# Recurrent mixer of a hybrid decoder layer: consumers of VectorE's drains wait on the drains' own counter

## What is computed

```python
a_mat = jnp.where(strict, jnp.einsum('bnhid,bnhjd->bnhij', k_beta, k) * decay, 0.0)
t_inv = lax.linalg.triangular_solve(eye + a_mat, eye, left_side=True, lower=True)
attn = jnp.einsum('bnhid,bnhjd->bnhij', q, k) * decay
def step(state, xs):
    v_new = u_c - jnp.einsum('bhik,bhkv->bhiv', w_c, state)
    o = jnp.einsum('bhik,bhkv->bhiv', q_c, state) + jnp.einsum('bhij,bhjv->bhiv', attn_c, v_new)
    state = state * jnp.exp(gl_c)[..., None, None] + jnp.einsum('bhik,bhiv->bhkv', k_c, v_new)
```

## Time and profile before

| | us |
|---|---|
| median of 3 runs | 597.84 |
| the runs | 596.25, 597.97, 597.84 |
| profiled execution, its own time | 597.7 |
| span of the profiled execution | 595.8 |
| TensorE matmul busy | 545.4 (92%) |
| VectorE busy | 390.1 (65%) |
| ScalarE busy | 322.1 (54%) |
| GpSimd busy | 221.1 (37%) |

### The profile page before, as it was taken

One profiled execution on the slowest core, in us unless ns is written; L12 is line 12 of the kernel. 1 busy time (PEld: TensorE's weight loads), 2 busy tenths in 40 slices (PEclk: granted clock), 3 DMA queues, 4 the chain that ended last, 5 costly groups with the idle time before them and its releaser, 6 DMA issues.

```text
span 595.8 us, 10710 instructions
## 1 busy us (share of the span) xinstructions
PE 545.4 (92%) x4087; PEld 308.0 (52%) x4087; DVE 390.1 (65%) x920; ACT 322.1 (54%) x573; POOL 221.1 (37%) x164
## 2 busy tenths in 40 slices
PE   2999999999999866999899998989899898999997
PEld 1644556543357532467466575645455465444443
DVE  6520388765498696876877768668797556687211
ACT  4555645355467962560922805586676768246320
POOL 0154453613046660352632630441321375154420
PEclk9999999999999996999999999999999999999999
DMA  9345865653124230220220210212211221172411
GB/s 316 114 125 137 167 96 162 189 164 89 56 54 125 75 107 33 72 72 2 73 72 2 64 45 2 59 49 72 72 36 38 70 72 37 36 282 72 142 53 54
DMA packets 31173, 52.93 MB, mean 89 GB/s; under 512 B 2743, under 2 KB 13329, under 8 KB 31121
## 3 DMA queue, kind: packets, MB, share of 16 engines
q1 hardware_dynamic: 30825, 51.68, 29.9%
q10 hardware_dynamic: 296, 0.55, 0.5%
HBM read 49.80 MB, written 2.42 MB: 88 GB/s over the span
## 4 chain that ended last, share of the span: by engine, by line
PE 68%; DVE 17%; ACT 7%; issue 5%; SPq 2%; DMA 1%; POOL 0%; DVEq 0%; ACTq 0%; PEldq 0%; POOLq 0%
PE bank L1690 13%; PE bank L1692 12%; PE bank L1691 12%; PE bank L1986 5%; PE bank L1988 5%; PE bank L1896 5%; PE bank L1990 5%; PE bank L1888 3%; PE bank L1726 3%; ACT stage L744 2%; PE bank L1832 2%; DVE bank L1266 1%; DVE early L1300 1%; DVE small L1297 1%; ACT late L966 1%
## 5 line engine op out<-in xcount | busy, mean ns | idle before, releaser
L532 POOL TENSOR_TENSOR w_lo<-stage,w_hi 128x1024 f16<-128x1024 f32 (+4 forms) x76 | 149.4, 1970 | 218.9 <-ACT w_hi L752 218.8
L752 ACT ACTIVATE w_hi<-stage 128x1024 f16<-128x1024 f32 (+4 forms) x76 | 74.5, 981 | 13.9 <-PE bank L1692 9.0
L1986 PE MATMUL bank<-hT_hi,w_hi 128*128 128x512 f16 x192 | 73.0, 380 | 1.7 <-PE bank L1990 0.9
L744 ACT ACTIVATE stage<-stage,small 128x512 f32<-128x512 f32 (+4 forms) x120 | 73.6, 663 | 0.7 <-DMA stage<-in_w_in 0.6
L1988 PE MATMUL bank<-hT_lo,w_hi 128*128 128x512 f16 x192 | 72.9, 380 | 0.3
L1990 PE MATMUL bank<-hT_hi,w_lo 128*128 128x512 f16 x192 | 72.8, 379 | 0.3
L1690 PE MATMUL bank<-w_hi,hT_hi 128*128 128x260 f16 (+4 forms) x192 | 61.4, 320 | 3.0 <-DVE hT_lo L1074 1.4
L1691 PE MATMUL bank<-w_lo,hT_hi 128*128 128x260 f16 (+4 forms) x192 | 61.0, 318 | 0.0
L1692 PE MATMUL bank<-w_hi,hT_lo 128*128 128x260 f16 (+4 forms) x192 | 61.0, 318 | 0.0
L1690 PE MATMUL bank<-hT_hi,w_hi 128*128 128x512 f16 (+1 forms) x128 | 48.0, 375 | 2.5 <-ACT work L735 1.4
L1691 PE MATMUL bank<-hT_lo,w_hi 128*128 128x512 f16 (+1 forms) x128 | 47.8, 373 | 0.0
(11 more groups left out here) (331 smaller groups left out, 1145.9 us busy)
## 6 DMA issues: line engine op xcount, KB each, us to landing
stage<-in_w_in SPq DMA_DIRECT2D x40, 512.0 KB, 3.6
stage<-in_c_phi_w SPq DMA_DIRECT2D x8, 512.0 KB, 4.1
stage<-in_w_branch SPq DMA_DIRECT2D x8, 512.0 KB, 3.8
stage<-in_w_out SPq DMA_DIRECT2D x8, 512.0 KB, 4.7
stage<-in_w_in SPq DMA_DIRECT2D x8, 260.0 KB, 2.8
strips<-rel_rows SPq DMA_DIRECT2D x8, 256.0 KB, 6.5
late<-in_x SPq DMA_DIRECT2D x1, 2048.0 KB, 9.1
out_x<-late SPq DMA_DIRECT2D x8, 256.0 KB, 2.0
```

What stands on the lines that cost most here:

```text
L532: gp.tensor_tensor(piece_view(w_lo[:, k % PAIRS, :], c), piece_view(stage[:, piece_at[c, j] % STAGES, :], c), piece_view(w_hi[:, k % PAIRS ...
L744: ins = nc.scalar.activation(full[:, r, :], full[:, r, :], ACT.Copy, scale=g_w[:, 2 * j + r:2 * j + r + 1])
L752: nc.scalar.activation(piece_view(w_hi[:, k % PAIRS, :], c), full, ACT.Copy).then_inc(hi_ready, 1)
L1986: mm(G.bank(g)[:, :], w[0], h[0], start=k == 0, stop=False)
```

## The change

`GD`, its list of names and `done` go. Each waiter now waits for the same drain on `v_drained` itself, through a table that turns the old names into those of the ring. VectorE no longer waits behind a drain, and raises nothing there. One wait is kept, as `taken`: in chunk 0, ahead of predicated copies that read `neg_nT`. In `level_zero` of a later chunk, `transposed_zero` (two predicated copies into `t_hT`, the second held) moves ahead of the two predicated copies into `t_h`, of which the last raises `v_drained` for `n`. All 98 calls of `done` go; the waits of TensorE, ScalarE and GpSimd keep their places.

```diff
-        GD = Steps(sem("deltanet_ready"), g_names)
+        drain_of = {"nnt": "kk", "attn": "qk", "tt0": "n", "t": "u", "tt": "ut", "resid": "ks", "kt": "vt", "vnew": "x2", "oraw": "o", "state": "st"}
+
+        def drained(eng, kind, *at):
+            eng.wait_ge(v_drained, V.filled((drain_of.get(kind, kind), *at)))
...
-                GD.wait(gp, ("oraw", c))
+                drained(gp, "oraw", c)
...
-                        GD.wait(act, ("tt", c, LEVELS - 2))
+                        drained(act, "tt", c, LEVELS - 2)
...
-            def done(name):
-
+            def taken(name):
                 ve.wait_ge(v_drained, V.filled(name))
-                ve.nop().then_inc(GD.sem, 1)
...
                 ve.tensor_tensor(neg_nT, bank4(("kk", c)), decay_n, ALU.mult).then_inc(v_drained, 1)
-                done(("kk", c))
                 ve.tensor_tensor(attnT[c % 2], bank4(("qk", c)), attnT[c % 2], ALU.mult).then_inc(v_drained, 1)
-                done(("qk", c))
                 if c == 0:
+                    taken(("kk", 0))
                     transposed_zero(0)
...
                 ps = bank4(("n", c))
+                if c:
+                    transposed_zero(c)
                 put(t_h, 0, ps[0:HALF, :, 0:HALF], 0, HALF)
                 put(t_h, 0, ps[HALF:P, :, HALF:P], HALF, P).then_inc(v_drained, 1)
-                if c:
-                    transposed_zero(c)
-                done(("n", c))
...
                     ve.tensor_copy(z_h[r0:P, :, :], ps[r0:P, :, :]).then_inc(v_drained, 1)
-                    done(("z", c, l))
...
                         put(t_h, l, halves4(("u", c, l))[0:r1, :, :], 0, r1).then_inc(v_drained, 1)
-                        done(("u", c, l))
                         put(t_hT, LEVELS - 1 + l, halves4(("ut", c, l))).then_inc(v_drained, 1)
...
-                    done(("ut", c, l))
...
-                    GD.wait(pe, ("z", c, l))
+                    drained(pe, "z", c, l)
                     if l > 1:
-                        GD.wait(pe, ("tt", c, l - 1))
+                        drained(pe, "tt", c, l - 1)
...
-                        GD.wait(pe, ("state", c - 1))
+                        drained(pe, "state", c - 1)
```

More of the change, by code:

```diff
@@ L671, in _ @@
                 if c < NT - 1:
-                    GD.wait(gp, ("z", c, LEVELS - 1))
+                    drained(gp, "z", c, LEVELS - 1)
                     reset(t_h)
-                    GD.wait(gp, ("tt", c, LEVELS - 1))
+                    drained(gp, "tt", c, LEVELS - 1)
                     gp.wait_ge(joined, c + 1)
@@ L934, in _ @@
                     if c > 1:
-                        GD.wait(act, ("oraw", c - 1))
+                        drained(act, "oraw", c - 1)
                     for h in range(4):
@@ L978, in _ @@
             drain_gate(11)
-            GD.wait(act, ("oraw", NT - 1))
+            drained(act, "oraw", NT - 1)
             for u, (m, q, h) in enumerate(units):
@@ L1381, in token_major @@
                 ve.tensor_tensor(v_tok, bank4(("vt", c)), heads(nk, c), ALU.mult).then_inc(v_drained, 1)
-                done(("vt", c))
             def decayed_products(c):
@@ L1523, in _ @@
                         ins.then_inc(v_drained, 1)
-                        done(("ks", c))
                         next(norm)
@@ L1537, in _ @@
                 ve.tensor_tensor(v_new, bank4(("x2", c)), heads(a_s, c), ALU.mult).then_inc(v_drained, 1)
-                done(("x2", c))
                 if c < NT - 1:
@@ L1550, in _ @@
                     ve.tensor_tensor(o_tok, ps, o_state, ALU.add).then_inc(v_drained, 1)
-                done(("o", c))
                 if c < NT - 1:
@@ L1560, in _ @@
                         ins.then_inc(v_drained, 1)
-                    done(("st", c))
                     token_major(c + 1)
@@ L1968, in within_b2 @@
                 if (t, k) == (3, 1):
-                    GD.wait(pe, ("nnt", 0))
+                    drained(pe, "nnt", 0)
                     transposes(("n", 0), [neg_nT[:, h, :] for h in range(4)])
@@ L2039, in _ @@
                 qc, kc_, vc_ = features(c)
-                GD.wait(pe, ("tt0", c))
+                drained(pe, "tt0", c)
                 for l in range(1, LEVELS):
@@ L2065, in _ @@
                         fill(FILL_U)
-                        GD.wait(pe, ("t", c, l))
+                        drained(pe, "t", c, l)
                 if c < NT - 1:
@@ L2070, in _ @@
                     fill(8)
-                GD.wait(pe, ("tt", c, LEVELS - 1))
+                drained(pe, "tt", c, LEVELS - 1)
                 pe.wait_ge(joined, c + 1)
@@ L2075, in _ @@
                     fill(FILL_X)
-                    GD.wait(pe, ("nnt", c + 1))
+                    drained(pe, "nnt", c + 1)
                     transposes(("n", c + 1), [neg_nT[:, h, :] for h in range(4)])
@@ L2081, in _ @@
                     compressed_out()
-                GD.wait(pe, ("vnew", c))
+                drained(pe, "vnew", c)
                 four(("o", c), lambda h: attnT[c % 2][:, h, :], lambda h: v_new[:, h, :])
```

## The result

| | before | after |
|---|---|---|
| median of five runs, us | 597.84 | 594.21 |
| the runs | 596.25, 596.75, 597.84, 597.93, 597.97 | 592.45, 592.9, 594.21, 594.43, 594.84 |
| profiled execution: own time, span | 597.7, 595.8 | 594.84, 592.9 |
| VectorE busy | 390.1 | 385.1 |

The ratio is 0.994, with a 95% interval of 0.9918 to 0.9963: faster by 3.6 us, where 2.1 was forecast.

A forecast was written before the change was run, and what follows sets the result against it. TensorE holds 68% of the chain, VectorE 17%; freeing VectorE pays only where it stands on the chain, in the recurrent stage. Five terms sum to 2.09 us, so 597.84 becomes 595.7, range 594.3 to 597.8.

The forecast's parts named there:

- The price of a `done`: VectorE's wait for its own drain plus a NOP costs 0.23 us if what follows waits for nothing else.
- Term 1: Two releases on the chain, first transposes before the stage and first `z` of chunk 0: 0.03 each, 0.06 us.
- Term 2: Chunk 0 to 1: `k_tok` starts earlier behind the state's copy, the first `z` waits for it: gain 0.20 us.
- rival B: Less won: the gap falls only to the held 0.04, 0.11 a piece, chunk 1 stays blocked; 597.0 us, chance 0.20.
- Term 3: Chunk 1, cumulative product and levels 3 to 5, where VectorE runs against GpSimd: gain 0.85 us (0.23 to 1.49).
- both blocked: Chunk 1: lines 1036 and 1424 stay held by GpSimd, only the level 4 `z` copy's `done` counts: 0.23 us.
- both escape: Chunk 1: lines 1036 and 1424 are no longer held by GpSimd, all is won: 1.49 us.
- Terms 4 and 5: Chunk 2's cumulative product gains 0.29 us; chunk 3, `resid` to level 3's `z` copy, three `done`s gain 0.69.
- rival A: More won: both blocked chunk 1 operations escape and the pause before 364.05 goes with the NOP; 594.7 us, chance 0.15.
- Rival C: VectorE's gap is the operation's own and stays; only releases gain, 0.03 at some eight places; 597.6 us, chance 0.14.
- Rival D: Slower: VectorE's earlier operations meet GpSimd's in a worse order in chunks 1 and 2; 600.8 us, chance 0.06.
- The margin of `st`: `level_zero`'s new order delays the drain of `n`, but hides before `st`'s loads with some 0.1 us left.

The follow-up runs named there:

- Which drains: Changed kernel with wait and NOP put back behind all drains but resid, z, u and state: 594.59 us; counterpart, put back behind only those: 596.43.

## Why the prediction was right and wrong

*The price of a `done`, 0.23.* Right behind `resid` and the `z` copies: -0.09 in after, and the three kernels split it into 0.11 for the wait and 0.12 for the NOP behind it.

*Term 1, releases.* The kernel with its `done`s kept and its consumers moved shows 0.06, as forecast.

*Term 2, `k_tok`.* 0.12 for 0.20. `k_tok` starts 0.03 behind the state's copy and not under it; here rival B's assumption holds. `v_tok` now also stands 0.03 behind `k_tok`, but for another reason: it waits for TensorE's transposes, which end at 276.90 + 0.66 = 277.56. After's timelines of TensorE and VectorE:

```profile
276.90 0.66 PE L1707 MATMUL bank<-consts,qkvT 128*128 128x128 f32 x4 [0.24 <-DVE late L1537]
277.60 0.69 DVE L1372 TENSOR_TENSOR work<-bank,small 128x512 f32<-128x512 f32 x1
```

In before, too, `v_tok` started 0.04 behind those transposes, so the row from which the prediction took its -0.08 could not show it. The value was right: in the kernel with the 48 freed the transposes end at 277.04, and `v_tok` at 277.43 starts 0.08 under the end of `k_tok`.

*Term 3, chunk 1.* The largest step inside the terms: 1.07 for 0.85, inside its bounds of 0.23 to 1.49. The middle was a compromise between "both blocked" and "both escape". What happened is one of each. Line 1031 was blocked in the place of 1036, line 1412 won its race. Of the 1.49, 0.42 stayed behind: the 0.32 above the floor at 293.50, and 0.09 that TensorE lost at a gate product before it. The margin of 0.02 is no luck of hundredths. In after line 1411 is itself held until GpSimd's operation ends, and 1412 gets in ahead of GpSimd's next; in the traces of all eight runs that keep GpSimd's order and where 1412 wins, it wins by 0.02.

*Terms 4 and 5.* 0.31 for 0.29 and 0.73 for 0.69, at the forecast loads.

*The step that failed: two pauses that the sum puts at nothing.* The sum took 0.23 a `done` and the releases, and nothing else. It left out 0.72 from two pauses of VectorE ahead of a put. The one at 364.05 was seen, and left to rival A with 0.15, as a thing that goes with the NOP. The one at 319.06 was not seen at all: its put is marked as waiting for TensorE, and chunk 2's levels had been read as standing at their floor, though the load there had 0.72 ahead of it. The runs showed in its place that these pauses do not belong to the `done`. With all 98 kept and one instruction more on the list, both are gone, 0.73 us; they stand at numbers 579 and 707 of VectorE's list, behind a wait or NOP by itself. The change takes 97 instructions off the list and moves both puts. That no other operation on the chain met such a number in its place is in part luck: the kernel with 48 freed lost 0.34 that way. With both pauses in the sum the forecast would have been 2.8 us, and 595.0. What such a pause is stays open.

*The rest, in small steps, 0.24 for 0.06.* In the kernel that keeps its `done`s the releases give 0.06, so 0.18 of it is VectorE's. It is not traced to single operations; one source can be the second put of a pair, which starts under the first one's end (0.84 for two puts where they took 1.03).

*From 3.2 to 3.6.* The stage gives 3.2. In the runs whose stage is shorter by 3.16 to 3.20, the medians differ from before's by 3.2 to 3.8, and in the repeat of after itself by 3.3. So the 0.4 beyond the stage is variation, most likely that ahead of the stage, and no gain of the change. Without it the time would have been inside the range.

*Rival C* falls: wait and NOP cost what they seemed to, the NOP alone nothing. *Rival B* holds at `k_tok`. *Rival A* was nearest, with its pause gone, though not by way of the NOP, and only one of its two blocked operations free. *Rival D*'s mechanism is real, with the sign turned: in the kernel with two NOPs it is the later VectorE that fell behind one more GpSimd operation in chunk 1 and lost the race of chunk 2, 1.5 us together. *The margin of `st`* was enough.

## What to carry to other kernels

A semaphore raised by the working instruction itself cost nothing that shows here: the next operation starts 0.08 us under its end. A wait placed on the producer's own sequencer so that it may raise another one costs 0.11 us for the wait and 0.12 for what is issued behind it, wherever that engine is on the chain. Look for gaps that are longer than others of the same kind before summing a per-item price, also where the view names another engine as the releaser. A change of a program's length moves such stalls by itself, so a control with one idle instruction more is worth its run. And the price of speeding an engine up is not that of slowing it down: 0.23 less per drain gave 2.4 us in the stage, 0.09 more took over 4, of which 1.5 was collisions and some new pauses.

## What the runs showed of the hardware

VectorE paused by 0.34 to 0.37 us ahead of instructions 451, 579, 707 and 835 of its list, 128 apart, waits and lone NOPs counted. It showed at six places in three programs, each time right behind a wait or a lone NOP. At 579 in the two kernels of "Which drains", behind a wait but with an operation still running, only 0.05 of it is left. At number 451 of the kernel with 13 NOPs, behind a working instruction, nothing showed; nor did it at 835 of the kernel with one instruction more, behind a wait and under an operation that still ran. One NOP more moved three of them off, and 0.73 us went. By the Trainium skill (Runtime: NRT & Kernel Launch, section Instruction fetch mechanics) an engine refills its instructions in blocks of 256 and the crossing is mostly hidden. A spacing of 128 does not agree with blocks of 256, and no run here shows whether these pauses are fetches.

Two operations of VectorE and GpSimd that meet: the one that starts first keeps its time, even by 0.02 us, and the other is stretched. It is 0.69 to 1.45 or 1.50 on VectorE, 1.05 to 1.58 on GpSimd, and 0.17 to 2.07 for line 1031, an operation with a single tensor of 128x4. The Trainium skill (GPSIMD Engine Reference, Key points) names two SBUF inputs or a 2-port perf mode as the condition. Line 1412 has two SBUF inputs, and the trace agrees. Line 1031 has one input and waited all the same; by the page it would have to run in such a mode, which no view here shows.
